# A transformer block in split float32: some weight units begin with one product of 512 columns, and the activation transposes move one unit on

## What is computed

```
h = rms_norm(x, norm_mix)
x = x + hybrid_mixer(h, ...)        # h @ w_in, three attention branches, gates, w_out
h = rms_norm(x, norm_ffn)
x = x + (silu(h @ w_gate) * (h @ w_up)) @ w_down      # width 5632
return rms_norm(x, norm_final)
```

## Time and profile before

| | before |
|---|---|
| median of 3 runs | 1376.24 us |
| the profiled execution's own time | 1378.64 us |
| its span | 1376.9 us |
| TensorE matmul busy, weight load busy | 99%, 96% |
| VectorE, ScalarE busy | 67%, 51% |
| granted TensorE clock | 0.999 |

### The profile page before, as it was taken

The page is one execution under the profiler, slowest core; times in us unless marked ns, Lnnn a source line. Parts: engine busy times, 40 slices in busy tenths (PEclk is TensorE's granted clock), DMA queues, the critical chain, the costliest instruction groups (busy, mean ns, idle before and its releaser), DMA issues.

```text
span 1376.9 us, 26434 instructions
## 1 busy us (share of the span) xinstructions
PE 1362.5 (99%) x11280; PEld 1325.5 (96%) x11280; DVE 922.5 (67%) x1192; ACT 702.5 (51%) x913; POOL 44.9 (3%) x70
## 2 busy tenths in 40 slices
PE   8999999999999999999999999999999999999997
PEld 7888999999999999999999999999999999999997
DVE  5554557667655657666787888875446778887554
ACT  6343356656545655465645554544334455545444
POOL 3000010000000110000000000000000000000111
PEclk9999999999999999999999999999999999999999
DMA  7776655444565666546556655565555565666653
GB/s 241 246 231 219 186 171 156 140 152 146 154 192 168 194 203 218 184 168 201 165 182 194 217 181 181 182 214 208 191 198 184 184 214 169 193 196 231 210 198 123
DMA packets 135264, 261.08 MB, mean 190 GB/s; under 512 B 8448, under 2 KB 25408, under 8 KB 134768
## 3 DMA queue, kind: packets, MB, share of 16 engines
q1 hardware_dynamic: 132912, 251.13, 57.0%
q0 software_dynamic: 1792, 7.57, 1.6%
q10 hardware_dynamic: 448, 0.76, 0.2%
HBM read 257.33 MB, written 2.10 MB: 188 GB/s over the span
## 4 chain that ended last, share of the span: by engine, by line
PE 88%; DVE 7%; ACT 2%; DMA 2%; issue 1%; ACTq 0%; DVEq 0%
PE bank L646 24%; PE bank L647 23%; PE bank L648 23%; PE bank L885 4%; PE bank L887 4%; PE bank L888 4%; DVE weight_lo_ring L1322 2%; PE bank L634 2%; DVE weight_sums_lo L1342 1%; ACT weight_hi_ring L1071 1%; DMA raw_ring<-in_w_up 1%; DVE weight_sums L1331 1%; PE bank L784 1%; DVE act_rows L1382 1%; PE bank L695 1%
## 5 line engine op out<-in xcount | busy, mean ns | idle before, releaser
L1322 DVE TENSOR_TENSOR weight_lo_ring<-raw_ring,weight_hi_ring 128x1024 fp32r<-128x1024 f32 (+2 forms) x479 | 579.9, 1221 | 319.2 <-ACT weight_hi_ring L1071 263.9
L1071 ACT ACTIVATE weight_hi_ring<-raw_ring 128x1024 fp32r<-128x1024 f32 (+2 forms) x431 | 446.2, 1047 | 343.4 <-PE bank L648 271.0
L646 PE MATMUL bank<-weight_hi_ring,hT_hi 128*128 128x256 f32 (+2 forms) x1276 | 380.9, 298 | 0.0
L648 PE MATMUL bank<-weight_hi_ring,hT_lo 128*128 128x256 f32 (+2 forms) x1276 | 375.5, 294 | 0.0
L647 PE MATMUL bank<-weight_lo_ring,hT_hi 128*128 128x256 f32 (+2 forms) x1276 | 375.5, 294 | 0.0
L646 PEld LDWEIGHTS bank<-weight_hi_ring,hT_hi 128*128 128x128 f32 x1276 | 239.8, 188 | 10.0 <-issue 3.4
L647 PEld LDWEIGHTS bank<-weight_lo_ring,hT_hi 128*128 128x128 f32 x1276 | 239.9, 188 | 6.1
L648 PEld LDWEIGHTS bank<-weight_hi_ring,hT_lo 128*128 128x128 f32 x1276 | 239.6, 188 | 6.3
L646 PE MATMUL bank<-weight_hi_ring,h2T_hi 128*128 128x256 f32 x704 | 196.5, 279 | 3.2 <-DVE weight_lo_ring L1322 3.1
L648 PE MATMUL bank<-weight_hi_ring,h2T_lo 128*128 128x256 f32 x704 | 195.3, 277 | 0.0
L647 PE MATMUL bank<-weight_lo_ring,h2T_hi 128*128 128x256 f32 x704 | 195.3, 277 | 0.0
(11 more groups left out here) (253 smaller groups left out, 1897.0 us busy)
## 6 DMA issues: line engine op xcount, KB each, us to landing
raw_ring<-in_w_in SPq DMA_DIRECT2D x96, 512.0 KB, 3.4
raw_ring<-in_w_gate SPq DMA_DIRECT2D x88, 512.0 KB, 4.3
raw_ring<-in_w_up SPq DMA_DIRECT2D x88, 512.0 KB, 4.2
raw_ring<-in_w_down SPq DMA_DIRECT2D x88, 512.0 KB, 3.9
raw_ring<-in_w_in SPq DMA_DIRECT2D x55, 480.0 KB, 4.2
raw_ring<-in_w_out SPq DMA_DIRECT2D x32, 512.0 KB, 4.0
raw_ring<-in_w_br_c SPq DMA_DIRECT2D x16, 256.0 KB, 3.9
raw_ring<-in_w_br_a SPq DMA_DIRECT2D x16, 256.0 KB, 6.8
```

Of the source, the lines that this page charges most:

```text
L646: pe.matmul(dst, x_hi, w_hi, start=opening, stop=False, skip_group_check=True)
L648: m = pe.matmul(dst, x_lo, w_hi, start=False, stop=last and k == UK - 1, skip_group_check=True)
L1071: act.activation(whi[:, s, :, 0:width(u)], raw[:, s, :, 0:width(u)], ACT.Copy)\
L1322: dve.tensor_tensor(lo, w, hi.bitcast(F32), ALU.subtract).then_inc(lo_ready, 1)
```

## The change

Two edits. A unit that is not `qkv` or `up` begins with one product of 512 columns (same stationary tile, hi by hi, both halves at once) where TensorE did other work after the unit before it, in place of the two hi by hi products of 256 columns of the first block and tile. And the activation transposes of block `i` stand after U0 of block `i + 1`, no longer before it; the two that stand in `down` units stay.

```diff
-ACT_T_AT = {AT[("down", (h, 0), 5) if i == b - 1 else ("gate", i + 1, 5)]: i
+ACT_T_AT = {AT[("down", (h, 0), 5) if i == b - 1 else ("up", i + 1, 0)]: i
...
+def other_work_after(u):
+
+    k = u - U_MIX
+    return (k in PREP_AT or k in SOFT_AT or k in PROBS_T_AT or k in VALUES_AT or k in STICK or u in ACT_T_AT
+            or any(k in (s, s + 2, s + 4) for s in MLP_AT)
+            or any(u in (merge_T_at(m), out_T_at(m)) for m in range(NC_D)))
...
-            def products(slot, lhs, pair, first, last, k0, width=W, tiles=tuple(range(TT)), halves=(0, 1), apart=False):
+            def products(slot, lhs, pair, first, last, k0, width=W, tiles=tuple(range(TT)), halves=(0, 1), apart=False, whole=False):
 
                 l_hi, l_lo = lhs
                 parts = [(h * Q4, (h + 1) * Q4) for h in halves] if width == W else [(0, width)]
+                if whole:
+                    pe.matmul(bank[2 * pair][:, :], l_hi[:, k0, 0:P], whi[:, slot, 0, :], start=first, stop=False,
+                              skip_group_check=True)
...
-                    pe.matmul(dst, x_hi, w_hi, start=opening, stop=False, skip_group_check=True)
+                    if not whole or k > 0 or t > 0:
+                        pe.matmul(dst, x_hi, w_hi, start=opening, stop=False, skip_group_check=True)
...
-                m = products(u % RING, lhs, q % 2, j == 0, j == n - 1, UK * j, width)
+                m = products(u % RING, lhs, q % 2, j == 0, j == n - 1, UK * j, width, whole=other_work_after(u - 1))
```

More of the change, by code:

```diff
@@ L937, in ffn_unit @@
                     pe.wait_ge(lo_ready, u + 1)
-                    products(u % RING, (h2T_hi, h2T_lo), 0, j == 0, j == UPC - 1, UK * j).then_inc(unit_used, 1)
+                    products(u % RING, (h2T_hi, h2T_lo), 0, j == 0, j == UPC - 1, UK * j,
+                             whole=other_work_after(u - 1)).then_inc(unit_used, 1)
                 elif what == "up":
@@ L963, in ffn_unit @@
                     products(u % RING, (actT_hi, actT_lo), c % 2, j == 0, j == n - 1, UK * j,
-                             apart=i == LAST_DOWN).then_inc(unit_used, 1)
+                             apart=i == LAST_DOWN, whole=other_work_after(u - 1)).then_inc(unit_used, 1)
             def last_units():
```

## The result

The change runs in 1384.07 us (median of 6 runs, 1383.88 to 1385.62) against 1376.2 us for the kernel before in the same session (1373.23 to 1379.15, 6 runs): ratio 1.0063, 95% interval 1.0053 to 1.0073. The forecast was 1367.6 us, with a range up to 1373.5. It was wrong in sign, by 16.5 us. A ratio here leaves out runs that are over 1.5% slower than the fastest of the same kernel; only experiment 12 has such runs.

The account below looks back on a forecast made before the run. TensorE's product stream, at two rates, plus waits for VectorE was taken as the bound. Terms of -4.6, -2.9, -1.1 and 0 gave -8.6 us: 1370.0 for the profiled execution, 1367.6 as median; range 1363.4 to 1373.5.

Parts of the forecast that it names:

- Term 1: At nine feed-forward places, moving the transposes removes most TensorE waits for VectorE: -4.6 us, bounds 5.6 and 2.
- Rival D: At g7, U2 and U0: the wait only moves, g7's gain being lost at the others; 1372.2 us, chance 0.15.
- Term 2: In units behind other work, the 512-column product brings the stream out at the fast rate: -2.9 us.
- Rival C: Behind the 71 units, the long product leaves the stream slow, always or at long reaches; 1408.5 us at worst, chance 0.1.
- Rival B: Behind long products nothing is reset; the rate is dealt as before, one in seven or so slow: 1370.5 us, chance 0.27.
- Term 3: At 71 places, one 512-column product costs less than two of 256: -1.1 us, between +0.2 and -2.1.
- Term 4: Thirteen slow units behind waits, 1.3 us, might go with the waits; counted as 0.

Follow-up runs that it names:

- experiment 12: The whole change, but with two 512-column products in a row instead of one at each of its places: 1373.54 us, ratio 0.9958 to the kernel before.
- experiment 1: Only the activation transposes moved, products as in the kernel before: 1371.69 us, ratio 0.9960 to that kernel.
- experiments 10 and 11: Transposes moved, rows of 1 to 12 products of 512 columns opening nine down units, in two different orders: 1379.67 and 1371.9 us, one run each.
- experiment 9: Transposes moved, with a single 512-column product in the whole kernel, in down's first half: 1378.59 us, ratio 1.0009 to the kernel before.
- experiment 3: The whole change, but each 512-column product made as two of 256 in the same order: 1371.73 us, ratio 0.9949 to the kernel before.
- experiment 4: Transposes moved, and all 48 down units of the first half made of 12 products of 512 columns: 1378.4 us, ratio 0.9997 to the kernel before.

## Why the prediction was wrong

**What bounds the kernel: right.** Two rates of one stream, 113.3 and 117.8 ns, and waits for VectorE; these two explain every profiled run in the table to 1.8 us.

**Term 1, the moved transposes, -4.6 us: right, and a little low.** 5.4 us by the waits of experiment 1, 5.9 in the change; the bound was 5.6 for all waits at the nine places gone, and that came true. The wait of 0.15 to 0.4 us that I left at U2 is there once in experiment 1 (0.4), and in the change it is under 0.05. VectorE's rows of the block at 1108 us, which answer to the earlier trace rows:

```profile
1111.68 1.22 DVE L1335 TENSOR_TENSOR weight_lo_ring<-raw_ring,weight_hi_ring 128x1024 fp32r<-128x1024 f32 x1
1112.82 1.28 DVE L1403 TENSOR_TENSOR actT_lo<-bank,actT_hi 128x512 fp32r<-128x512 f32 x2
1114.01 0.95 DVE L1355 TENSOR_TENSOR weight_sums_lo<-weight_sums,weight_sums_hi 128x768 fp32r<-128x768 f32 x1
```

`actT_lo` stands behind a split, and the 0.77 us for which VectorE idled ahead of L1342 are gone, filled by it, as worked out. Rival D, the wait that moves, is refuted.

**Term 2, slow units behind other work, -2.9 us: this is the step that failed.** I took it that the stream comes out of a long product at the fast rate, because "the next load is over before it is wanted, whatever rhythm the transposes left", and leaned on 25 entries behind long attention products of which 24 ran fast. Three things were wrong. The count left out the one entry of that trace where a row of 256-column products at 216 ns stands directly ahead of a unit, and it ran slow, with the two units behind it (unit 104):

```profile
314.04 1.99 PE L810 MATMUL bank<-probs_T,vc_block_diagonal 128*128 128x256 f32 x8
315.69 0.47 PE L646 MATMUL bank<-weight_hi_ring,hT_hi 128*128 128x256 f32 x1
```

Behind L838 and L695 stand products of 128 columns before the unit begins. The entries counted lie behind two or more products of another kind (256 columns at 215 ns), and the change puts in one of 512; inside a fast stream that number decides (experiments 10 and 11). Whether it is why those entries ran fast was not tried. And what decides is no slack in the loads: a single long product inside an undisturbed fast stream turned it slow (experiment 9), though the load of its successor, from 942.20 to 942.39 us, was over before that began at 942.42: the premise held there and the conclusion didn't. Instead of -2.9 us the term was +12.6. Behind eight transposes a single long product turned the stream over, whichever way, at 15 of the 19 such entries of the change: at four behind transposes of `merged`, and at all eleven behind activation transposes. The four behind transposes of `x`, at 594, 617, 640 and 662 us, came fast and stayed fast, and no run shows why. The eleven entries of the change at 718, 761, 805, 848, 891, 933, 1108, 1153, 1195, 1240 and 1280 us came slow, fast, slow, fast, fast, slow, fast, slow, fast, slow, fast and left the opposite. Eight transposes alone kept a fast stream fast, 17 times of 17 in experiment 1. Fast stretches were the rule, so turning over lost far more than it gained.

**Rival C** comes nearest, in its weaker form (the slow rhythm at long reaches, not always): 33 of the 71 long products left the stream slow, and there are 121 slow units more: by its own formula 1376.2 - 5.7 + 121 x 0.107 = 1383.4, against 1384.07 measured. The 0.1 that I gave it was too little; the case for it was on the page, in that every disturbance in the trace could turn the rate either way, and I had made one nearest row stand for the length of a product when it differed in their number too. **Rival B**, dealt as before, is refuted by experiment 3, where two short products in the same place leave 12 slow units in the mixer, and the long one 59.

**Term 3, the product itself, -1.1 us: too favourable.** In a row it takes 233.3 ns, above my bound of 229; alone inside a fast stream 225, even with two short ones. Behind transposes:

```profile
805.10 0.48 PE L649 MATMUL bank<-weight_hi_ring,h2T_hi 128*128 128x512 f32 x1
805.42 0.28 PE L659 MATMUL bank<-weight_lo_ring,h2T_hi 128*128 128x256 f32 x1
805.54 0.28 PE L660 MATMUL bank<-weight_hi_ring,h2T_lo 128*128 128x256 f32 x1
```

The successor starts 318 ns behind it, where two short ones in that place take 202 + 121 = 323 (experiment 1, starts from 1100.59 us); but the first product of the second tile starts 783 ns behind it, against 780 with short ones. The term is about 0. The Trainium skill, page "TensorE: Matmul & The Clock Gate", section "Back-to-back issue gap", gives N / 2.4 + 2.5 ns for an isolated warm matmul, 215.8 for 512 columns and 109.2 for 256, and some 131 ns at 512 columns for a stream in which each matmul has its weight load. The trace agrees with neither: in such a stream products of 256 columns keep no pace under 113.3 ns here, and none of 512 is followed in less than 225. The prediction used the first figure for such a stream and didn't name the second.

**Term 4, luck behind waits, 0:** not a term that can be left at 0 in one execution. A wait at unit 224 or 225 (673 to 679 us) that ends in the slow rate is carried for 14 units to the next transposes, and in experiment 12 to the end of the kernel.

## What to carry to other kernels

Before trusting a small edit to a saturated stream, read the pitch of its instructions stretch by stretch: here one instruction of another length slowed every one behind it by 4% until a later disturbance, and the cost reached more than 150 us beyond the edit. Change the place of other work and the shape of products in separate versions; here the move alone is the version to keep (1371.69 us, ratio 0.996 to the kernel before), and the change loses more than twice what it gains. When a nearest row is used for an operation that the trace doesn't have, check that it agrees in number and surroundings as well as in size.

## What the runs showed of the hardware

Products of 256 columns with a weight load each run at one of two steady rates, at the same clock: 113.3 ns, and 117.8 ns where every row of the timeline is 281 ns long instead of 276. A stream keeps its rate until something disturbs it: for 59 units (1416 products) in experiment 9. Inside a fast stream one or three products of 512 columns in a row turned it slow, and two, four, six or twelve left it fast (13 cases, two and six once each); a slow stream follows no such rule. Not shown is why. The starts in the traces suggest a beat: in fast stretches the step is 17 times 6.667 ns and nearly all starts fall within some 1.5 ns of one phase of that interval throughout the kernel before, in slow ones three products take 53 times 6.667 ns (353.3) and the starts go through three phases; a row of long products steps by 231 and 236 ns in turn, 70 such intervals a pair. That is worked out from starts alone, and no run tested it otherwise. Nor does parity cover every case: in experiment 4 a row of 504 long products behind transposes ended in the slow rate.
